# A hybrid SSD, attention and expert block on one core: branches by quarters of tokens, later row pieces, half outputs

## What is computed

```python
h = modulate(layer_norm(x), sh1, sc1); hc = modulate(layer_norm(xc), csh1, csc1)
z, xbc, dtr, q, k, v, g = split_projection(h @ w_in)      # and the same of hc
xbc = silu(depthwise_conv_centred(xbc, conv_w, conv_b))
y_ssd  = rms_norm((scan_both_directions(xbc, dtr) + d_skip * xs) * silu(z), norm_w)   # 2048 wide
y_attn = windowed_attention(rope(q), rope(k), v, kc, vc, sink)                         # 1024 wide
m = sigmoid(g_ssd) * (y_ssd @ w_ssd_br) + sigmoid(g_attn) * (y_attn @ w_attn_br)
y = m @ w_o + b_o
x = layer_norm(ALPHA * x + g1 * y) * ln1_g + ln1_b
h = modulate(layer_norm(x), sh2, sc2)
aff = softmax(h @ w_router)                 # 16 experts, each takes its 128 best tokens
moe[idx] += gate_vals * ((silu(xs @ w_g) * (xs @ w_u)) @ w_down)
out = layer_norm(ALPHA * x + g2 * moe) * ln2_g + ln2_b
```

## Time and profile before

| | us |
|---|---|
| time, median of 3 (lowest to highest) | 2876.5 (2875.23 to 2880.35) |
| the profiled execution: time | 2879.5 |
| its span | 2877.8 |
| TensorE busy | 2466.0 (86%) |
| VectorE busy | 1644.7 (57%) |
| ScalarE busy | 1051.9 (37%) |
| GpSimd busy | 543.0 (19%) |
| mean DMA rate | 193 GB/s |

### The profile page before, as it was taken

How to read it: one execution, slowest core, us unless ns; L and a number is a source line. 1 busy time by engine, 2 the same in 40 slices (tenths; PEclk the granted TensorE clock), 3 DMA queues, 4 the chain that set the end, 5 groups by cost and what they waited for, 6 DMA issues and landing times. The chain is left out here.

```text
span 2877.8 us, 30935 instructions
## 1 busy us (share of the span) xinstructions
PE 2466.0 (86%) x11820; PEld 1961.4 (68%) x11820; DVE 1644.7 (57%) x1720; ACT 1051.9 (37%) x1332; POOL 543.0 (19%) x420
## 2 busy tenths in 40 slices
PE   7899999969989996994999939879683599999992
PEld 2788887757779875673666538668573488888881
DVE  6454544443315773783555452443455699999994
ACT  4233332211113111551333431221233377777772
POOL 0100000021001441895000000000143112222213
PEclk8999999989999998996999969989896799999996
DMA  5333333345434784976345244554333599999994
GB/s 206 110 111 118 111 118 100 124 162 190 154 111 153 271 299 154 313 272 164 61 91 104 44 134 132 163 151 142 123 117 148 216 373 393 397 397 399 398 358 146
DMA packets 305022, 555.83 MB, mean 193 GB/s; under 512 B 22245, under 2 KB 208965, under 8 KB 281545
## 3 DMA queue, kind: packets, MB, share of 16 engines
q1 hardware_dynamic: 274778, 438.51, 44.7%
q0 software_dynamic: 25184, 108.37, 11.6%
q10 hardware_dynamic: 4944, 7.41, 0.9%
HBM read 435.26 MB, written 118.71 MB: 192 GB/s over the span
## 5 line engine op out<-in xcount | busy, mean ns | idle before, releaser
L2488 DVE TENSOR_TENSOR e_wlo<-e_w,e_whi 128x2048 fp32r<-128x2048 f32 x188 | 425.8, 2289 | 42.8 <-ACT e_whi L2441 41.7
L2441 ACT CAST e_whi<-e_w 128x2048 fp32r<-128x2048 f32 x192 | 366.3, 1916 | 121.9 <-PE e_gu L2601 82.8
L445 PE MATMUL f_lat<-h_hi,w_hi 128*128 128x512 f32 x800 | 256.2, 401 | 31.9 <-DVE w_lo L598 31.9
L445 PE MATMUL f_lat<-h_lo,w_hi 128*128 128x512 f32 x800 | 251.7, 396 | 0.0
L445 PE MATMUL f_lat<-h_hi,w_lo 128*128 128x512 f32 x800 | 251.5, 395 | 0.0
L445 PEld LDWEIGHTS f_lat<-h_hi,w_hi 128*128 128x128 f32 x800 | 136.6, 190 | 65.6 <-DVE w_lo L598 33.7
L2019 PE MATMUL b_acc<-b_hi,b_whi 128*128 128x512 f32 x384 | 151.4, 394 | 14.0 <-DVE b_lo L1970 14.0
L445 PEld LDWEIGHTS f_lat<-h_lo,w_hi 128*128 128x128 f32 x800 | 136.8, 189 | 27.6
L445 PEld LDWEIGHTS f_lat<-h_hi,w_lo 128*128 128x128 f32 x800 | 136.7, 189 | 27.7
L1665 PE MATMUL a_c_ps<-a_prob,a_v 128*128 128x512 f32 x304 | 155.5, 595 | 0.0
L1740 DVE CUSTOM_DVE_ANT_0 a_masked<-a_a_ps,a_mask 128x640 f32<-128x640 f32 x128 | 105.4, 825 | 81.8 <-PE a_a_ps L1638 77.5
(11 more groups left out here) (343 smaller groups left out, 5451.0 us busy)
## 6 DMA issues: line engine op xcount, KB each, us to landing
e_w<-in_w_gate_up SPq DMA_DIRECT2D x128, 1024.0 KB, 10.4
e_w<-in_w_down SPq DMA_DIRECT2D x64, 1024.0 KB, 8.8
w_raw<-in_w_in SPq DMA_DIRECT2D x50, 512.0 KB, 4.0
t_space<-xbcT POOLq DMA_DIRECT2D x18, 1280.0 KB, 6.8
before<-t_space SPq DMA_DIRECT2D x16, 1024.0 KB, 4.1
y_before<-before SPq DMA_DIRECT2D x64, 256.0 KB, 6.4
xbcF<-f_out POOLq DMA_DIRECT2D x24, 640.0 KB, 3.5
xbcT<-t_out POOLq DMA_DIRECT2D x24, 640.0 KB, 4.4
```

The lines of the kernel that those rows point to most:

```text
L445: mm = nc.tensor.matmul(o, weights[:, b, k, :], part[:, k, a:a + n], start=(k == 0 and n_pass == 0), stop=(k == KT - 1 and n_pass == 2))
L2441: nc.scalar.copy(whi[:, slot % SPLIT], w[:, slot]).then_inc(w_hi, 1)
L2488: V.tensor_tensor(wlo[:, slot % SPLIT], w[:, slot], whi[:, slot % SPLIT].bitcast(F32), ALU.subtract).then_inc(w_split, 1)
```

## The change

It has six parts. (1) In the gates, the row pieces begin three gates later, rows are kept and stored one or two gates later than that, and the stores of the gates are awaited by the states stage instead of at the end of the block. (2) Attention no longer awaits its last store; ScalarE squares, and VectorE scales, the first two tiles of the branches in attention's tail. (3) The branches go by quarters of 256 tokens: 4 x 8 units of 72 matmuls with 256 columns, written out without loops. The weights are loaded again in each quarter, in half pieces (768 KB) into three buffers; the next quarter's tokens are squared, scaled, turned, weighed and split between the units of the running one. Stores of m are awaited where the residual stage loads them. (4) In the residual stage the first product goes by column halves, the split of tile 0 stands between weight pieces, row DMAs are issued by GpSimd instead of ScalarE, the last tile's bias and shift are on VectorE, and the affinities go through TensorE straight into an SBUF tile that the experts read. (5) Gathers and scatters use the token table directly; the last expert's down product, y and scatter go by column halves, the rows of `moe` are loaded half by half inside the expert block, and VectorE measures the left halves there. (6) The output stage measures the right halves; GpSimd adds five biases and VectorE three; SyncE stores five tiles and ScalarE three.

The core of the diff:

```diff
-        SUM_AFTER = {4: 0, 7: 1, 10: 2, 13: 3}
-        PER_GATE = 3
+        SUM_AFTER = {5: 0, 8: 1, 10: 2, 13: 3}
+        PER_GATE, FROM_GATE = 3, 3
...
-                    if n - 2 in SUM_AFTER:
-                        store_rest(SUM_AFTER[n - 2])
+                    if n - 4 in SUM_AFTER:
+                        store_rest(SUM_AFTER[n - 4])
...
-                    for j in range(PER_GATE * n, min(PER_GATE * n + PER_GATE, PARTS)):
+                    for j in range(max(PER_GATE * (n - FROM_GATE), 0), min(PER_GATE * (n - FROM_GATE) + PER_GATE, PARTS)):
                         add_part(j)
-                    if n - 1 in SUM_AFTER:
-                        keep_row(SUM_AFTER[n - 1])
+                    if n - 2 in SUM_AFTER:
+                        keep_row(SUM_AFTER[n - 2])
...
-                    pool.wait_ge(gate_out[b], 16 * NG // 2)
...
+    def wait_gates(self, eng):
+        for b in range(2):
+            eng.wait_ge(self.gate_out[b], 16 * (2 * D // P) // 2)
...
+                ahead.wait_gates(sp)
                 load_w(1)
...
-                sp.wait_ge(cols_out, 16 * LCHUNK)
...
+                for n in range(2):
+                    act.wait_ge(later.y_first[n], 16)
+                    if n:
+                        act.wait_ge(later.squared, n)
+                    nc.scalar.activation(a_ps[:].rearrange("p b n -> p (b n)"), later.y[:, n], ACT.Square, accum_out=later.ssq[:, n:n + 1]).then_inc(later.squared, 1)
+                    act.wait_ge(later.mean_step, 2 * n + 2)
+                    nc.scalar.activation(later.root[:, n:n + 1], later.mean[:, n:n + 1], ACT.Sqrt).then_inc(later.rooted, 1)
...
+                inverse_mean(0)
                 invert(LCHUNK - 1)
+                scale(0)
+                inverse_mean(1)
+                scale(1)
                 for g in range(G):
...
+    QUARTERS = 4
+    NW = SEQ // QUARTERS
...
+    RAWS = 3
+    SQUARE_AT, SCALE_AT, TURN_AFTER, FULL_AT, HI_AT, LO_AT, ATTN_AT = (0, 1), (1, 2), (2, 4), (3, 5), (3, 5), (4, 6), (0, 5)
+    Y_AT, A_AT = (3, 5), (1, 6)
...
+                def load_piece(p):
+                    f = (p // 2) % FT
+                    if p >= RAWS:
+                        sp.wait_ge(w_split, p - RAWS + 1)
+                    if p % 2 == 0:
+                        sp.dma_start(raw[p % RAWS], ssd_v[:, 0:KP, f * P:f * P + P]).then_inc(w_in[p % RAWS], 16)
+                    else:
+                        sp.dma_start(raw[p % RAWS][:, 0:KY - KP], ssd_v[:, KP:KY, f * P:f * P + P]).then_inc(w_in[p % RAWS], 16)
+                        sp.dma_start(raw[p % RAWS][:, KY - KP:KP], attn_v[:, :, f * P:f * P + P]).then_inc(w_in[p % RAWS], 16)
...
+                load_a(0)
+                load_a(1)
+                load_gates(0)
+                sp.wait_ge(later.a_out, 16 * LCHUNK)
+                load_piece(2)
+                load_y(2)
+                load_piece(3)
+                load_y(3)
+                load_a(2)
+                load_a(3)
...
+                    if g and 2 * g + 3 < 2 * UNITS:
+                        load_piece(2 * g + 3)
+                    if 2 * g + 4 < 2 * UNITS:
+                        load_piece(2 * g + 4)
+                    if g + 1 < UNITS:
+                        load_gates(g + 1)
+                    if q + 2 < QUARTERS:
+                        for t, n in next_tiles(q + 1):
+                            if f == Y_AT[t]:
+                                load_y(n)
+                            if f == A_AT[t]:
+                                load_a(n)
+                    if q == QUARTERS - 1 and f in (1, 2, 3, 4):
+                        if f == 1:
+                            sp.wait_ge(y_lo, LCHUNK)
+                            sp.wait_ge(a_split, LCHUNK)
+                        later.load_wo(s, sp, f - 1)
 
...
+                split_lo(0)
+                split_lo(1)
+                for n in range(2):
+                    weigh(n)
+                    attn_lo(n)
+                    ssd_lo(n)
+                for g in range(UNITS):
+                    q, f = divmod(g, FT)
+                    if g + 1 < UNITS:
+                        split_lo(2 * g + 2)
+                        split_lo(2 * g + 3)
+                    for t, n in next_tiles(q):
+                        if f == SQUARE_AT[t]:
+                            inverse_mean(n)
+                        if f == SCALE_AT[t]:
+                            scale(n)
+                        if f == FULL_AT[t]:
+                            weigh(n)
+                        if f == LO_AT[t]:
+                            ssd_lo(n)
+                        if f == ATTN_AT[t]:
...
+                def product(g):
+                    b, at = g % 2, NW * ((g // FT) % 2)
+                    pe.wait_ge(w_split, 2 * g + 1)
+                    if g >= 2:
+                        pe.wait_ge(m_made, g - 1)
+                    for k in range(KW):
+                        if k == KP:
+                            pe.wait_ge(w_split, 2 * g + 2)
+                        for n_pass, (weights, part) in enumerate(((whi, hi), (whi, lo), (wlo, hi))):
+                            mm = nc.tensor.matmul(acc[:, b, int(k >= KY), 0:NW], weights[:, b, k, :], part[:, k, at:at + NW],
+                                                  start=(k in (0, KY) and n_pass == 0), stop=(k in (KY - 1, KW - 1) and n_pass == 2))
+                    mm.then_inc(used, 1)
...
+                pe.wait_ge(later.const_in, 32)
+                turn(0)
+                turn(1)
+                for q in range(QUARTERS):
+                    pe.wait_ge(a_split, 2 * q + 2)
+                    pe.wait_ge(y_lo, 2 * q + 2)
+                    for f in range(FT):
+                        product(q * FT + f)
+                        for t, n in next_tiles(q):
+                            if f == TURN_AFTER[t]:
+                                turn(n)
...
+                    if n % 2 == 0:
+                        for b in range(2):
+                            sp.wait_ge(later.m_out[b], 64 * (n // 2) + 64)
...
-                pe.wait_ge(w_split, 4)
-                for n in range(LCHUNK):
+                pe.wait_ge(m_split, 1)
+                for c in range(2):
+                    pe.wait_ge(w_split, 2 * c + 2)
+                    for k in range(KT):
+                        for n_pass, (part, weights) in enumerate(((mhi, whi), (mhi, wlo), (mlo, whi))):
+                            mm = nc.tensor.matmul(acc[:, 0, 512 * c:512 * c + 512], part[:, 0, k, :], weights[:, k, 512 * c:512 * c + 512],
+                                                  start=(k == 0 and n_pass == 0), stop=(k == KT - 1 and n_pass == 2))
+                mm.then_inc(multiplied, 1)
+                for n in range(1, LCHUNK):
...
+                pe.wait_ge(aff_made, 2)
+                for n in range(LCHUNK // 2):
+                    nc.tensor.matmul(tp[0:2 * EXPERTS, n, :], sided[:, n, :], ident[:], start=True, stop=False)
+                    mm = nc.tensor.matmul(tp[0:2 * EXPERTS, n, :], sided[:, LCHUNK // 2 + n, :], ident[:], start=False, stop=True)
...
-                    if n == 0:
-                        for j, row in ((G1, mod[0:1, 2 * D:3 * D]), (B_O, s.x["b_o"]), (LN_G, s.x["ln1_g"]), (LN_B, s.x["ln1_b"]),
-                                       (SC2, mod[0:1, 4 * D:5 * D]), (SH2, mod[0:1, 3 * D:4 * D])):
-                            act.dma_start(rowv[:, j], row.to_broadcast([P, D])).then_inc(rows_in, 16)
-                for n in range(2):
-                    split_hi(n)
+                    if n == 1:
+                        split_hi(0)
+                split_hi(1)
...
+                    if n == LCHUNK - 1:
+                        dve.wait_ge(scaled1, LCHUNK)
+                        V.tensor_tensor(x1[:, n % 2], x1[:, n % 2], rowv[:, LN_B], ALU.add).then_inc(last_x1, 1)
...
+                keep_logits(LCHUNK - 2)
+                dve.wait_ge(scaled2, LCHUNK)
+                V.tensor_tensor(h2[:, (LCHUNK - 1) % 2], h2[:, (LCHUNK - 1) % 2], rowv[:, SH2], ALU.add).then_inc(last_h2, 1)
+                keep_logits(LCHUNK - 1)
...
+    def load(self, eng, moe, c, tiles):
+        for n in tiles:
+            eng.dma_start(self.x[:, n, 512 * c:512 * c + 512], moe[n * P:n * P + P, 512 * c:512 * c + 512]).then_inc(self.half_in[c][n], 16)
...
+                for c in range(2):
+                    sp.wait_ge(half_out[c], 16)
+                    tail.load(sp, moe, c, range(0, LCHUNK, 2))
...
+                for c in range(2):
+                    cols = slice(512 * c, 512 * c + 512)
+                    dve.wait_ge(down_half, c + 1)
+                    V.scalar_tensor_tensor(y[:, 1, cols], down[:, cols], gatec[:, 0:1], g2[:, cols], ALU.mult, ALU.mult).then_inc(y_half, 1)
+                for n in range(LCHUNK):
+                    dve.wait_ge(tail.half_in[0][n], 16)
+                    V.bn_stats(tail.stats[:, n, 0, :], tail.x[:, n, 0:512]).then_inc(tail.measured, 1)
...
```

(8 more changed lines are left out.)

520 lines of the change are left out of this document (270 added, 250 removed).

## The result

| | us |
|---|---|
| before, median of 4 | 2877.28 (2875.23 to 2880.35) |
| after, median of 4 | 2771.81 (2770.57 to 2772.97) |
| ratio | 0.963, 95% interval 0.9618 to 0.9643 |
| profiled execution after: time, span | 2772.97, 2771.3 |

The change makes the kernel 3.7% faster. The forecast was 2758, its range 2744 to 2782. The spans of the two profiled executions differ by 106.5 us, where the sum of the terms gave 118.1.

A forecast was written before the change was run, and what follows sets the result against it. TensorE, busy 86% of the span, was taken to bound the kernel through six waits, with experts also full on DMA. Terms summed to -118.1 us from 2877.8, span 2759.7, median forecast 2758; range 2744 to 2782.

The forecast's parts named there:

- The gates: Gates: row pieces moved three gates later let weight splits run on time; TensorE's 31.9 us waits and 3.1 low clock go, -35.0.
- The head of the branches: Branch block's start to first product: 43.8 us become 18.0, with squares and scaling of two tiles in attention's tail, -25.8.
- The products: Branch products: 309.1 us become 289.6, as 2304 matmuls at 0.120 us plus turns and low clock, -19.5.
- quicker narrow matmuls: Rival, branch products: 256-column matmuls take down to 0.109 us instead of 0.120, giving 2733; chance 0.04.
- the end of the span: Output stage: left half of y and its statistics lie in VectorE's idle time, 19.7 us left for VectorE, -14.2.
- between branches and residual: Change from branch to residual block: the last merge's store is no longer awaited, -3.5, bounds -2 to -4.
- attention's end: Change from attention to branch block: the last store's way to memory is no longer awaited, -3.0, bounds -2.3 to -4.
- the end of the gates: Change of block behind the gates: the row's store is still awaited, so 9.9 us stay; 0, bounds +2 to -6.
- the experts: Expert stage: first gather issued without a copy of indices ahead of it, steady experts stay full, -1.0.
- The ends give less: Rival: successive scatters land later and first split waits for gates' stores, +5 to +12, so 2767; chance 0.09.
- The slower one: Rival, branch units: three-piece weight ring does not cover its latency, 3.7 us more a unit decides, 2898; chance 0.02.
- The bound of units by DMA: Rival, branch units: loads (or VectorE) bound them at 9.3 us instead of 8.64, +21, so 2779; chance 0.15.

The follow-up runs named there:

- the run with the gates alone: Kernel before with only the gates' row pieces three gates later, rows kept and stored later, every block-end wait left: 2843.73 us, ratio 0.9872.
- the one-batch kernel: Changed kernel with rows awaited in states stage, last m store by SyncE, residual loads ahead of stores, output tiles in one batch of eight: 2735.7 us, ratio 0.9492.

## Why the prediction was right, and where it was not

The direction, the place of every large term and the range were right. The measured 2771.8 us lie 14 above the forecast of 2758, near the upper end of the bounds of the terms. The three largest terms, which hold 80 of the 118 us, came within 1.5 each. The gates rested on two waits and on the clock that was granted behind them, and the run with the gates alone shows that nothing else was in it. The head of the branches rested on a row of durations in series with its waits. The products rested on 0.120 us from another stage with the same number of columns; a unit took 72 x 0.120 to the hundredth, so the rival of quicker narrow matmuls is out. For head and products no run takes a part of the change away; what speaks for them is that the head lasts 43.8 us in both traces without the part and 18.2 or 18.3 in all twelve with it.

**Mis-sized, the end of the span.** The mechanism (left halves in idle time) was right, the term was 14.2 and measured 7.8. The step that failed is the list of what is left for VectorE, 19.7 us from the first right half. From 2742.86 to 2768.25 it is 25.4. The small instructions are three sets with each its own wait for ScalarE's root (one such row took 1.47 us in the trace of before as well), some 4.2 us where I wrote "some 1.7"; VectorE waits 1.3 us for ScalarE's first tile of the last batch, a row that stood in the earlier trace rows and that I left out; and the first bias takes 3.13 instead of 1.2. These three are 5.7 of the missing 6.4.

The way from y's right half to the first statistics, which the sum took over as 14.8 us, came to 15.3, but by two things that cancel. The two scatters of the halves:

```profile
L2834 POOL DMA_INDIRECT moe<-e_y,e_half_rows x2: 1541/1541/1541, 2723.8 to 2729.1; - x2
...
DMA to landing us min/median/max: 5.0/7.3/9.6
```

The second, issued beside the eight loads of the left halves, took 9.6 us to land, the first 5.0 (the last one before: 6.2). Against that the right halves are loaded inside the expert block, so that the first statistics follow 1.0 us behind the block's start instead of 3.5. The prediction named later scatters in its rival and had no row for them; whether the loads delay this one was not tested.

**Mis-sized, between branches and residual.** "No longer awaits the store" was priced at 3.5 and was worth 1.4, of which 0.6 are the narrower merge and its handing over to GpSimd. The step took the gap for the landing of a store, and had nothing for GpSimd's drain behind it. Issuing that store from SyncE shows what it was.

**Mis-sized, attention's end.** The term of 3.0, taken from another store of the span, measured 4.1: from the last store's issue to the branch block 1.3 us instead of 5.2. Here SyncE is the last to leave, and what is left is short.

**Right for a partly wrong reason, the end of the gates.** The zero held, but I bounded the gain of a full move by 6 us, and it is 7.5: I thought of the stores, which land in 2, and the 5.6 us of drain stood in no row of mine.

**Small.** The affinities' way through TensorE saved 2.6 of the 3.9 forecast, and the experts, from the search to the last y, took 0.9 more instead of 1.0 less. Executions of the same expert code differ by more than that (612.8 to 616.5 us), so whether the term is there stays open. Of the 3.2 us in stretches that the change does not touch, 1.6 lie before the first gate, no more than two executions differ by (616.1 to 618.3), and 2.1 are the states stage at its lower clock; some 0.5 come back around it.

**Signs and bounds.** Two of the signs named in advance did not come: TensorE's wait for turns fell to 16.9 us and not below 10, since its 13.4 us ahead of the block were not counted, and VectorE ended 25.4 us after its first right half and not 20. One sign of being wrong did come, an output block more than 12 us behind the last product (14.3). The late scatter stands in it; but the right halves' loads, which used to stand behind the block's start, now lie ahead of it, and the first statistics, which the sum counts, came only 0.4 us late. The lower bounds of the terms add up to 2743 and not 2745.

**The rivals.** "The ends give less", 2767, is nearer to the measured time than the forecast is: the end of the span gives 6.4 less. Of its two reasons the later scatter cost 0.4 net, and the first split behind the gates waits for nothing; what was lost lies behind them. The slower one needed 3.7 us more per unit: with a buffer less it was 0.66. The bound of units by DMA needed more traffic than there was: half a megabyte more per unit cost 6.5 us in all.

## What to carry to other kernels

When a wait is taken from the end of a stage, look which engine comes last to the change of block without it, and at the DRAIN records there: here GpSimd's were the long ones, so its last work belongs well ahead of the block's end, and the last store on SyncE. In a queue that works in order, ask for the next tile's inputs ahead of the stores that wait for this tile's result; the sign is an engine that waits for a load which was issued right behind a store. A list of what is left for an engine has to count its sets of small instructions and its waits for its partner from the rows, not as a round remainder.

## What the runs showed of the hardware that I had not expected

GpSimd's DRAIN at a change of block lasts 5.6 to 7.7 us at the end of the gates and 1.5 to 3.3 at the end of the branches, and when GpSimd is the last to leave, all engines wait for it. It has no fixed price behind a wait for a store: 5.6 in one block and 1.5 in the other. Where SyncE is the last, the next block begins 0.4 to 0.7 us after the end of its issue (1944.33 to 1944.75, 789.44 to 789.97, 1635.66 to 1636.33).

VectorE's addition of a bias, with both inputs in SBUF, ends about 1.1 us after GpSimd's instruction has ended (2762.38 and 2763.45; in the one-batch kernel three in a row of 2.1 to 2.5 us instead of 1.22), while gains with one input in PSUM keep their 1.22 us beside it (2759.06). The Trainium skill (SBUF — State Buffer, SBUF: two separate sides) tells of an exclusive lock between the two engines, held for a whole instruction, that two inputs in SBUF need; the rows agree.

The DMA engines moved 309 GB/s in packets of mostly 512 bytes to 2 KB while TensorE worked at full clock beside them, at a busy share above 1: the share is no measure of what room is left.
